# TensorE waits once a stage for its own last product, in a float32 two-block transformer kernel

## The reference

```
for l in range(2):                                   # first block
    qkv, gates = rmsnorm(x) @ w_in[l]                # three attention branches a, b, c
    y = sum(sigmoid(gate) * (o_branch @ w_up))       # over the three branches
    x = x + y @ w_out[l]
    x = x + cross_attention(rmsnorm(x), mem, ...)    # w_q_x, w_kv_x, w_o_x
    x = x + (silu(g) * u) @ w_down[l]                # g, u = rmsnorm(x) @ w_gu[l], width 2816 each
for i in range(2):                                   # second block, 256 tokens and 256 of context
    x = x + mod * swiglu(modulate(x), ffn_a_in[i], ffn_a_out[i])
    x = x + mod * mixer_i(modulate(x))               # i = 0: windows and Hyena; i = 1: retention
    x = x + mod * swiglu(modulate(x), ffn_b_in[i], ffn_b_out[i])
```

## The kernel before, in words

| stage | columns | products, L1123 and the first block | wide from about |
|---|---|---|---|
| gu and down, layer 0 | 256 | 1584 | 411 us |
| gu and down, layer 1 | 256 | 1584 | 982 us |
| ffn a, i = 0 | 512 | 3168 | 1187 us |
| ffn b, i = 0 | 512 | 3168 | 1878 us |
| ffn a, i = 1 | 512 | 3168 | 2247 us |
| ffn b, i = 1 | 256 | 1584 | 2941 us |

## Time and profile before

### The profile page before, as it was taken

One profiled execution on the slowest core, in us unless ns is written; L12 is line 12 of the kernel. 1 busy time (PEld: TensorE's weight loads), 2 busy tenths in 40 slices (PEclk: granted clock), 3 DMA queues, 4 the chain that ended last, 5 costly groups with the idle time before them and its releaser, 6 DMA issues.

```text
span 3129.9 us, 55500 instructions
## 1 busy us (share of the span) xinstructions
PE 2963.4 (95%) x23214; PEld 2792.9 (89%) x23214; DVE 1967.7 (63%) x3143; ACT 1234.9 (39%) x2095; POOL 219.7 (7%) x300
## 2 busy tenths in 40 slices
PE   8898989999898998999998889999999998999899
PEld 7788889978797998999986689999999998987899
DVE  5755778565567857767575557666566656435665
ACT  4454554435455444222344323223322223235443
POOL 1311000022100000000011120000000001000000
PEclk8999999999999998999999999999999999999999
DMA  5434457533355763555231114444354443242454
GB/s 195 129 108 135 149 181 245 191 117 101 115 172 166 248 210 128 177 181 168 95 125 39 55 54 149 162 156 148 103 167 156 154 143 115 85 144 89 134 191 141
DMA packets 245596, 447.65 MB, mean 143 GB/s; under 512 B 14483, under 2 KB 87076, under 8 KB 244580
## 3 DMA queue, kind: packets, MB, share of 16 engines
q1 hardware_dynamic: 239584, 430.79, 42.5%
q10 hardware_dynamic: 5764, 13.33, 1.3%
HBM read 443.01 MB, written 1.05 MB: 142 GB/s over the span
## 4 chain that ended last, share of the span: by engine, by line
PE 81%; DVE 9%; ACT 5%; issue 3%; POOL 1%; DMA 0%; ACTq 0%; DVEq 0%; SPq 0%; POOLq 0%
PE ps L1123 64%; DVE split L1820 3%; ACT split L1527 2%; PE ps L1151 2%; PE ps L1153 2%; PE ps L1152 2%; DVE A L1817 1%; ACT A L1617 1%; PE ps L1098 1%; PE ps L1099 1%; PE ps L1057 1%; PE ps L1102 1%; DVE AR L1820 1%; DVE small L1988 1%; PE ps L1276 1%
## 5 line engine op out<-in xcount | busy, mean ns | idle before, releaser
L1123 PE MATMUL ps<-AR,split 128*128 128x256 f32 x19392 | 2319.9, 280 | 25.6 <-DVE A L1817 9.2
L1123 PEld LDWEIGHTS ps<-AR,split 128*128 128x128 f32 x19392 | 2263.7, 190 | 72.8 <-issue 34.8
L1820 DVE TENSOR_TENSOR split<-raw,split 128x1024 fp32r<-128x1024 f32 (+2 forms) x728 | 807.6, 1151 | 647.9 <-ACT split L1527 639.7
L1527 ACT ACTIVATE split<-raw 128x1024 fp32r<-128x1024 f32 (+2 forms) x728 | 682.5, 986 | 825.0 <-PE ps L1123 702.2
L2060 DVE SCALAR_TENSOR_TENSOR junk<-A,cb 128x1024 bf16<-128x1024 f32 x144 | 175.6, 1220 | 43.5 <-DMA A<-w_modT 41.3
L2060 DVE SCALAR_TENSOR_TENSOR A<-A,cb 128x1024 f32<-128x1024 f32 x144 | 175.3, 1217 | 0.0
L2296 POOL TENSOR_TENSOR A<-A 128x256 f32<-128x256 f32 (+1 forms) x45 | 39.8, 884 | 1665.3 <-ACT A L1537 1658.0
L1820 DVE TENSOR_TENSOR AR<-A,AR 128x256 fp32r<-128x256 f32 (+2 forms) x252 | 138.1, 549 | 23.1 <-ACT AR L1591 7.8
L1579 ACT ACTIVATE AR<-A 128x256 fp32r<-128x256 f32 (+1 forms) x132 | 68.4, 526 | 191.6 <-DVE A L1910 191.6
L1817 DVE SCALAR_TENSOR_TENSOR A<-A,ps 128x256 f32<-128x256 f32 (+1 forms) x196 | 95.7, 505 | 64.7 <-ACT A L1575 59.8
L1575 ACT ACTIVATE A<-ps 128x256 f32<-128x256 f32 (+1 forms) x132 | 63.9, 489 | 143.3 <-PE ps L1123 142.7
(11 more groups left out here) (230 smaller groups left out, 2233.1 us busy)
## 6 DMA issues: line engine op xcount, KB each, us to landing
A<-w_modT SPq DMA_DIRECT2D x144, 512.0 KB, 4.5
raw<-w_in SPq DMA_DIRECT2D x120, 512.0 KB, 4.5
raw<-w_gu SPq DMA_DIRECT2D x80, 512.0 KB, 4.8
raw<-ffn_a_in SPq DMA_DIRECT2D x80, 512.0 KB, 4.4
raw<-ffn_b_in SPq DMA_DIRECT2D x80, 512.0 KB, 4.4
raw<-ret_in SPq DMA_DIRECT2D x48, 512.0 KB, 4.2
raw<-w_down SPq DMA_DIRECT2D x44, 512.0 KB, 5.0
raw<-ffn_a_out SPq DMA_DIRECT2D x44, 512.0 KB, 4.4
```

The source lines that it names most:

```text
L1123: mm = e.matmul(out[:, s:s + NT], wt[:, c, m_], xs(k0 + c, a + s, a + s + NT), start=first and part + s == 0, stop=last and part == 2 and ...
L1527: e.activation(hi, self.raw_view(q), ACT.Copy).then_inc(*self.mark(("w hi", q)))
L1820: return self.e.tensor_tensor(out, v, hi.bitcast(F32), ALU.subtract)
```

## The change

TensorE counts the products of a stage. The first block of a stage sets the count and arms one mark, 288. In front of every later block of a projection in the group `WIDE` the new `settle` compares the count with the mark, and the first time that it is reached TensorE waits for the last product of the block before. Nothing else is changed: the same products in the same order, the same loads and the same work on the other engines.

```diff
+SETTLE = (288,)
...
     def start(self):
         e = self.e
+        self.streak, self.marks = 0, []
         e.wait_ge(*self.after("ones"))
...
+    def settle(self, i, products):
+
+        if self.marks and self.streak >= self.marks[0]:
+            self.marks.pop(0)
+            self.e.wait_ge(*self.after(("used", i - 1)))
+        self.streak += products
...
                     self.catch_up()
                     yield
+                self.streak, self.marks = 3 * (k0 + nk) * (n // P) * (T // NT), list(SETTLE)
                 continue
+            if group is WIDE:
+                self.settle(i, 3 * nk * (n // P) * (T // NT))
             for m in range(n // P):
```

## The result

The changed kernel takes 3173.56 us (median of 20 runs, 3141.27 to 3190.5), the kernel before 3150.68 us (20 runs beside them, 3129.1 to 3164.6). The ratio is **1.0066, 95% interval 1.0042 to 1.0089**: slower by 0.66%, some 21 us. The profiled execution of after took 3183.85 us, with a span of 3181.7; that of before has 3129.9. The two profiles are thus 51.8 us apart, more than twice the distance of the medians. Both numbers need an explanation.

A forecast was written before the change was run, and what follows sets the result against it. TensorE bounds the kernel, its wide stages being unbroken rows of products at 0.1133 us. Eight waits, 2.6 us, and one long stage slow, 13.0 us, add 15.6 to 3130.27: 3146 us, range 3131 to 3172.

The forecast's parts named there:

- all the short ones: SwiGLU stages with 256 columns turned slow behind their waits, counted as 11.6 us in the range's upper end.
- Counts and places: Eight waits, one in each of six SwiGLU stages and one per layer in mixing; 2880 or 1296 products behind the SwiGLU marks.
- Price of one wait: At each new wait TensorE loses 0.22 us before the next product and 0.11 behind it: 0.33 us, 2.6 for eight.
- The two paces: TensorE's products start every 0.1133 or 0.1178 us, 4.5 ns apart; each pace goes on by itself and changes at a restart.
- the row taken as a fast restart: Row of products behind an idle time at 877.90 us, counted as one of four fast restarts among six.
- No one queued behind it, clock untouched: Only TensorE's next load and product stand behind each wait; other engines lose nothing and the clock stays 1.00: no charge.
- One in three, independent: Each restart of TensorE comes back slow with one chance in three, from two slow of six restarts in the trace.
- every break comes back slow: Rival: all eight waits leave TensorE in the slow pace, 2.6 + 57 = 60 us, 3190 us; chance 0.10.
- all stay fast: Rival: all long stages stay fast behind the waits, costing 2.6 us, or 8.4 with one short stage slow; chance 0.36.
- One long stage slow: One of three 512-column SwiGLU stages turns slow: 13.0 us, 15.6 with the waits; one stage had 44%.
- Before, all six stages are in the fast pace where the mark falls, so the break can't win anything there: At the marks of the six SwiGLU stages the break can only draw the pace again, for all products up to the next norm.
- The context's sums as a limit in layer 1: In layer 1's 256-column stage the sums break the row anyway, leaving 948 products behind the mark, 4.3 us if slow.

The follow-up runs named there:

- experiment 5: The changed kernel once more, with no edit, against the kernel before: 3161.21 us (9 runs), ratio 1.0073; its profiled execution took 3147.56 us.
- experiment 2: Changed kernel with TensorE's wait for its own last product ahead of every block from 288 products on, 199 waits in all: 3216.2 us (one run).
- second kind: Executions, of whatever kernel, in which nine products of the third branch's keys in layer 0 take 1.11 us; seven of the 14 profiles.
- first kind: Executions, of whatever kernel, in which nine products of the third branch's keys in layer 0 take 1.09 us; seven of the 14 profiles.
- experiments 1 to 8: The first eight follow-ups, on the changed kernel, edited or not; the first of them waited for the block before last: 3148.93 us, ratio 1.0028.
- experiment 4: Changed kernel with the mark at 1056 products in place of 288: 3141.81 us (10 runs), ratio 1.0001 against the kernel before.
- experiment 6: Changed kernel with the mark at 192 and a constant product of 256 columns behind the wait: 3149.56 us (12 runs), ratio 1.0011 against the kernel before.
- 7 and 8: Changed kernel with one wait in each SwiGLU stage at differing counts, 192 to 864 products, none in mixing: 3171.46 and 3177.52 us (one run each).
- experiments 3, 6, 9 and 10: Changed kernel with constant products at the breaks: nine forms by turns, 3242.19 and 3234.05 us; 256 columns at mark 192, 3149.56; nine other forms, 3318.61.
- experiments 3 and 9: Changed kernel with one of nine breaks by turns at each block from the mark (wait, constant product or both): 3242.19 and 3234.05 us.

## Why the prediction was right, and where it was not

The time and the sign were right: slower, 0.5% forecast (15.6 of 3130.27), 0.66% measured. That the size came so near is in part luck: the forecast took one long stage as turned, and what happens is nearly all or nearly nothing by execution, with a mean not far from one stage. The absolute 3173.56 lies a hair above the range's upper end, 3172, for two reasons. The base had moved: the prediction stood on three runs at 3130.27, and twenty give 3150.68. And "all the short ones" was summed as 11.6 us, which is two of them; the three are 5.8 + 4.3 + 5.8 = 15.9, which puts the end at 3177. Step by step:

- **Counts and places:** right. 2880 and 1296 products behind the marks, six breaks in the SwiGLU stages.
- **Price of one wait, 0.33 us:** right. Start to start, the product behind the break comes 333 or 334 ns after the last one and the next 221 or 222 ns behind it in the six stages of after, where 113 each were due: 0.22 + 0.11.
- **The two paces, 4.5 ns apart, each kept by itself:** right for the SwiGLU stages, and to the hundredth. Elsewhere it isn't: the row taken as a fast restart, 877.90 with 89 products, was cut by its window at 888 us, and just there the block of `up c` begins, at 118.3 ns, without a restart. 2880 products take 326.49 us in experiment 5 and 339.26 in after; the forecast had 326.4 and 339.3. Each of the long stages lost 13 to 14 us.
- **No one queued behind it, clock untouched:** right. The clock is 1.00 around the break. The Trainium skill ("TensorE: Matmul & The Clock Gate", section "A second HAM failure mode: psum-queue depth-cycling") tells of another kernel in which small idle times between groups of matmuls made the clock fall and rise, and the prediction named that as a rule against this change. Here 199 breaks of 0.33 us did not bring such a fall: the clock is 1.00 in the 300 us window of experiment 2.
- **"One in three, independent": this step failed.** It took the pace behind a break for a draw at each break. The runs show a rule in its place: the outcome follows from the pace before the break, the form of the break and the kind of the execution. In the second kind all six stages of after turned at once. So the case "every break comes back slow", which had a chance of 0.10, is what happens in the SwiGLU stages of an execution of the second kind when they begin fast, and "all stay fast" (0.36) what happens in one of the first. "One long stage slow", the likeliest by the prediction, lies between the two; in neither profile of the changed kernel did the break turn one long stage alone (experiment 5 has one slow, which had begun so). The reason given for the rival, "it is the same eight times over", came nearest, but the outcome is a turn-over and not a slow pace, and it is the same in the six stages and not in `mixing`.
- **"Before, all six stages are in the fast pace where the mark falls, so the break can't win anything there":** wrong beyond the one profile. In 16 of 84 stages of the 14 profiles the stage reached its mark slow (or began slow, where it has no break). In the second kind the wait turns these fast. That lowers the mean price.
- **The context's sums as a limit in layer 1:** right in effect. The slow pace goes on behind them, over 348 products, but before had 331 products at that pace there too, so that only 17 are new.

**The sum as it stands now,** an estimate. With 0.19 of the stages slow at their mark, an execution of the second kind pays (0.81 - 0.19) x 54.9 = 34.0 us for the paces, one of the first kind about nothing. With half of the executions of each kind, 17.0 + 2.6 for the waits = 19.6 us, against 0.66% of 3150.68 = 20.8 measured. The half is the share among 14 profiles, so it is loose, and so is the 0.19: by kind the slow beginnings are 11 of 42 in the first and 5 of 42 in the second, and with the latter's 0.12 the estimate is 23.5 us. The twenty times of after fit two kinds: eight lie from 3141 to 3163, then none for 8 us, then the rest from 3171 up. The nine of experiment 5 show no such gap (one is at 3165.6). The runs without a profile have no mark of the kind, so this is a fit and not a proof. Slow beginnings would also be enough for the spread of before itself, 35 us: each long stage that begins slow costs 3072 x 4.5 ns = 13.8 us.

**What stays open.** What makes an execution of one kind or the other, and what the paces are inside TensorE, no run shows. It is not the program (after and experiment 5) and not the chip: experiments 1 to 8 ran on one, and three of their profiles are of the second kind. That the own wait's position is without effect is shown for 192 to 864 products and, in experiment 2, for every block; experiment 4, at 1056, was profiled in the first kind alone. Its ten times, 3128 to 3152 us, are a doubt: with the pace turned at 1056, an execution of the second kind would stand some 0.62 x 36 = 22 us higher, and with half of them so the ratio would be near 1.004, above the interval's end of 1.0034. Either its runs were nearly all of the first kind, or a wait so late in an unbroken stream doesn't turn the pace; this is not settled. Why half of experiment 6's runs were 20 us longer isn't settled either: a slow stage ahead of the mark or slow narrow stages would do it, but the profile caught a quick one.

## What to carry to other kernels

Where an engine is busy without a gap, ask at which pace, and read it from count and length of the row, not from the mean of one instruction: a standstill of 0.3 us can put thousands of instructions behind it on another pace, and here that cost, in the profile of after, twenty times the standstills themselves. A single profile shows one execution; before a small effect is drawn from it, profile the same kernel twice, and look for a row ahead of the change by which the executions differ. And a base of three runs can lie 20 us off when a kernel's executions differ as these do.

## What the runs showed of the hardware

- The product of 128x128 by 128x256 in the SwiGLU stages has two stable paces at the full clock, 113.3 and 117.8 ns start to start, each kept for up to 3072 products. The blocks of `up c` have a third, 118.3 ns, for 48 products at a time, entered and left without idle time of TensorE. No stream was faster than 113.3 ns. The Trainium skill ("TensorE: Matmul & The Clock Gate", section "Wait — 56ns, not 53.3ns?") gave, as the prediction's estimate, 109.2 ns; no row of the 14 profiles agrees with it.
- A wait for one's own last product costs 0.33 us and turns the pace over in some executions (six stages of six in after, every SwiGLU block in experiment 2, twelve marks of twelve in 7 and 8) and not in others of the same program (four fast stages of experiment 5). A constant product between the wait and the stream changes what comes out: with 256 columns a SwiGLU stage was fast behind it in experiments 3, 6, 9 and 10 each time; with 16 or 64 columns, in experiments 3 and 9, a fast stream turned slow, and a slow one nearly always fast.
- A constant product without a wait in front of it never changed the pace in experiments 3 and 9 (66 times of 66 in 3). In the SwiGLU stages no pace changed without a standstill; behind `up c` it did.
